# A hybrid decoder step on one core: inverse roots from a table, the last products on two engines, projection copies on ScalarE, and gathers of activations issued earlier

## The reference, cut to what matters

```
h = RMSNorm(x);  q, k, v, gates = h @ w_in
x += (sigmoid(gate_a) * attention @ w_a + sigmoid(gate_r) * retention @ w_r) @ w_o
h2 = RMSNorm(x)
x += PEER(h2)          # 128*128 = 16384 experts; 8 heads * 16 picks per token:
                       #   a = gelu(u[pick] . h2) * gate;  x += sum a * v[pick]
x += sigmoid(RMSNorm(x) @ w_ple_gate) * (p @ w_ple_proj)     # p: 256 wide
y = RMSNorm(x)
```

## Time and profile before

| | us |
|---|---|
| median of 3 runs (4647.2 to 4655.68) | 4655.38 |
| the profiled execution, its own time | 4651.09 |
| span from its first to its last instruction | 4649.5 |
| PE busy | 4572.7 (98%) |
| DVE busy | 2908.9 (63%) |
| ACT busy | 1241.7 (27%) |
| POOL busy | 1410.9 (30%) |
| mean granted TensorE clock | 0.994 |

### The profile page before, as it was taken

The page is one execution under the profiler, slowest core; times in us unless marked ns, Lnnn a source line. Parts: engine busy times, 40 slices in busy tenths (PEclk is TensorE's granted clock), DMA queues, the critical chain, the costliest instruction groups (busy, mean ns, idle before and its releaser), DMA issues.

```text
span 4649.5 us, 83246 instructions
## 1 busy us (share of the span) xinstructions
PE 4572.7 (98%) x33321; PEld 4501.8 (97%) x33321; DVE 2908.9 (63%) x4977; ACT 1241.7 (27%) x1636; POOL 1410.9 (30%) x1038
## 2 busy tenths in 40 slices
PE   8999999999999999999999999999999999999997
PEld 8999999989999999999999999999999999999997
DVE  7743442334425789556666525665659999999844
ACT  4113332133223122221111121212223333332332
POOL 1000000010000014443333324244147777665300
PEclk9999999999999999999999999999999999999999
DMA  6553345455544444245555478788868899999422
GB/s 216 162 168 113 115 153 170 151 164 165 176 152 131 145 134 143 104 141 172 173 170 176 169 248 277 270 303 290 313 255 334 330 373 383 377 372 352 185 81 90
DMA packets 538040, 976.03 MB, mean 210 GB/s; under 512 B 46027, under 2 KB 388315, under 8 KB 505947
## 3 DMA queue, kind: packets, MB, share of 16 engines
q1 hardware_dynamic: 185200, 471.13, 29.5%
q0 software_dynamic: 72304, 355.95, 19.8%
q10 hardware_dynamic: 280368, 146.70, 11.0%
HBM read 924.94 MB, written 230.82 MB: 249 GB/s over the span
## 4 chain that ended last, share of the span: by engine, by line
PE 89%; DVE 4%; issue 2%; DMA 2%; POOL 1%; ACT 1%; ACTq 0%; another core or an unknown queue 0%; DVEq 0%; SPq 0%; POOLq 0%
PE PS L2065 66%; PE PS L2563 18%; PE PS L2513 1%; DVE acc L1906 1%; DVE w_lo L1171 1%; DMA rows_y<-v_rows,row_iy 1%; POOL a_y L669 1%; DVE PS L1866 1%; DMA w_raw<-in_w 0%; PE PS L2457 0%; PE PS L2173 0%; ACT w_hi L761 0%; PE PS L2199 0%; ACTq L796 0%; DVE h_lo L1195 0%
## 5 line engine op out<-in xcount | busy, mean ns | idle before, releaser
L2065 PE MATMUL PS<-h_hi,w_hi 128*128 128x288 f32 x7808 | 2328.0, 298 | 31.0 <-DVE w_lo L1171 18.7
L2065 PE MATMUL PS<-h_lo,w_hi 128*128 128x288 f32 x7808 | 2306.1, 295 | 0.9 <-issue 0.9
L2065 PE MATMUL PS<-h_hi,w_lo 128*128 128x288 f32 x7808 | 2306.0, 295 | 0.7 <-issue 0.6
L2065 PEld LDWEIGHTS PS<-h_hi,w_hi 128*128 128x128 f32 x7808 | 1470.0, 188 | 62.9 <-issue 35.9
L2065 PEld LDWEIGHTS PS<-h_hi,w_lo 128*128 128x128 f32 x7808 | 1471.5, 188 | 1.0 <-issue 1.0
L2065 PEld LDWEIGHTS PS<-h_lo,w_hi 128*128 128x128 f32 x7808 | 1471.2, 188 | 1.4 <-issue 0.5
L761 ACT ACTIVATE w_hi<-w_raw 128x1024 fp32r<-128x1024 f32 x522 | 553.4, 1060 | 2438.2 <-PE PS L2065 2314.5
L1171 DVE TENSOR_TENSOR w_lo<-w_raw,w_hi 128x1024 fp32r<-128x1024 f32 x372 | 458.8, 1234 | 765.5 <-ACT w_hi L761 727.1
L625 POOL TENSOR_TENSOR w_lo<-w_raw,w_hi 128x1024 fp32r<-128x1024 f32 x152 | 379.0, 2493 | 1030.3 <-ACT w_hi L761 1030.3
L699 POOL DMA_INDIRECT a_el<-act_scr,act_i x192 | 322.6, 1680 | 58.9 <-issue 58.2
L1906 DVE SCALAR_TENSOR_TENSOR acc<-rows,a_sel,acc 128x2048 f32<-128x2048 f32 x128 | 301.1, 2353 | 3.9 <-POOL row_x L729 2.8
(11 more groups left out here) (353 smaller groups left out, 5375.1 us busy)
## 6 DMA issues: line engine op xcount, KB each, us to landing
w_raw<-in_w SPq DMA_DIRECT2D x652, 512.0 KB
v_rows<-in_w ACTq DMA_DIRECT2D x512, 256.0 KB, 3.8
v_raw<-in_w SPq DMA_DIRECT2D x128, 512.0 KB
act_scr<-gsp POOLq DMA_DIRECT2D x128, 288.0 KB
gate_scr<-g_st POOLq DMA_DIRECT2D x12, 2048.0 KB, 8.6
gl<-act_scr SPq DMA_DIRECT2D x20, 640.0 KB
fu_a<-act_scr SPq DMA_DIRECT2D x19, 640.0 KB
fu_g<-gate_scr SPq DMA_DIRECT2D x19, 640.0 KB
```

Of the source, the lines that this page charges most:

```text
L2065: ins = mm(dst[:, a], w[:, m, at + n], xx[:, k, a * TH:(a + 1) * TH], start=first and n == 0 and r == 0, stop=last and n == len(ks) - 1 an ...
```

## The change

Five edits:

1. Roots. In `root(2)` and `root(3)` ACT computes `Abs_reciprocal_sqrt` in place of `Sqrt`, and DVE's reciprocal goes; the three Newton instructions stay. In `root(3)` a fourth instruction writes the same result into PSUM as well, ahead of the one that writes `rstd2` and raises the new semaphore `rooted`.
2. Last products. DVE multiplies tiles 0 to 11, with the factor read from PSUM; POOL multiplies tiles 12 to 15, with the factor from SBUF. SP stores the pairs in the order 0, 1, 6, 2, 3, 7, 4, 5.
3. Projection copies. DVE copies the even tiles, ACT the odd ones (semaphore `p_done`), and PE waits for each by its own semaphore. ACT's splits stand at k = 1, 3, 5, 9 in place of 4, 8, 12, 15; DVE's low parts move up with the fewer copies.
4. Picks 32 to 47 are issued in iterations 96 and 97 in place of 97 and 98.
5. Within every POOL iteration of chunks 76 to 127 the picks come ahead of the rows in place of behind them. The iterations that have both are 84 to 87, 100 to 103 and 106 to 109, with four picks each.

```diff
 PICK_AT = {80: (0, 8), 81: (8, 16), 84: (16, 20), 85: (20, 24), 86: (24, 28), 87: (28, 32),
-           97: (32, 40), 98: (40, 48), 100: (48, 52), 101: (52, 56), 102: (56, 60), 103: (60, 64),
+           96: (32, 40), 97: (40, 48), 100: (48, 52), 101: (52, 56), 102: (56, 60), 103: (60, 64),
            106: (64, 68), 107: (68, 72), 108: (72, 76), 109: (76, 80), 110: (80, 84), 111: (84, 88)}
...
-            for n in range(KD // 2):
-                sp.wait_ge(S["yd"], 2 * n + 2)
+            for n in (0, 1, 6, 2, 3, 7, 4, 5):
+                if n < 6:
+                    sp.wait_ge(S["yd"], 2 * n + 2)
+                else:
+                    sp.wait_ge(S["yp"], 2 * n - 10)
                 sp.dma_start(o["y"][:, 2 * n:2 * n + 2], x[:, 2 * n:2 * n + 2]).then_inc(S["out"], 16)
...
                 put_gated(t)
+                for n in range(*PICK_AT.get(t, (0, 0))):
+                    pick_y(n)
                 for n in range(NY):
                     if Y_AT[n] == t + 1:
...
-                for n in range(*PICK_AT.get(t, (0, 0))):
-                    pick_y(n)
...
+            pool.wait_ge(S["rooted"], 2)
+            for k in range(KD - 4, KD):
+                pool.wait_ge(S["xl"], k + 1)
+                nc.gpsimd.tensor_tensor(x[:, k], x[:, k], rstd2[:], ALU.mult).then_inc(S["yp"], 1)
...
                 square(2, k)
-                if k in (4, 8, 12, 15):
-                    split(B_PG + 1 + (k + 1) // 4)
+                if k < KD // 2:
+                    n = 2 * k + 1
...
+                    nc.scalar.activation(halves(proj[:, n]), ring_a(n), ACT.Copy).then_inc(S["p_done"], 1)
+                if k in (1, 3, 5, 9):
+                    split(B_PG + 2 + (1, 3, 5, 9).index(k))
             split(B_PG + 6)
             split(B_PG + 7)
             act.wait_ge(S["ms"], 3)
-            nc.scalar.activation(rstd2[:], rms2[:], ACT.Sqrt).then_inc(S["rt"], 1)
+            nc.scalar.activation(rstd2[:], rms2[:], ACT.Abs_reciprocal_sqrt).then_inc(S["rt"], 1)
...
                 dve.wait_ge(S["rt"], 3 if r == 2 else 5)
-                inverse_root(rstd2, rms2)
+                ch.did(v.scalar_tensor_tensor(rms2[:], rms2[:], -0.5, rstd2[:], ALU.mult, ALU.mult))
+                ch.wait()
+                ch.did(v.tensor_tensor(rms2[:], rms2[:], rstd2[:], ALU.mult))
+                ch.wait()
+                if r == 3:
+                    ch.did(v.scalar_tensor_tensor(PS[:, 2:4, 0:TH], halves(rms2[:]), 1.5, halves(rstd2[:]), ALU.add, ALU.mult))
+                v.scalar_tensor_tensor(rstd2[:], rms2[:], 1.5, rstd2[:], ALU.add, ALU.mult).then_inc(S["rooted"], 1)
+                dve.wait_ge(S["rooted"], r - 1)
...
-            for n in range(KD):
+            for n in range(0, KD, 2):
                 projected(n)
-                if n >= 3 and n % 2 == 1:
-                    low_part((n - 3) // 2)
-                if n in (5, 9, 13):
+                if n >= 2:
+                    low_part(n // 2 - 1)
+                if n in (4, 8, 12):
                     split(B_PG + 2 + n // 4 - 1)
...
             root(3)
-            for k in range(KD):
+            ch.wait()
+            for k in range(KD - 4):
                 dve.wait_ge(S["xl"], k + 1)
-                v.tensor_tensor(x[:, k], x[:, k], rstd2[:], ALU.mult).then_inc(S["yd"], 1)
+                v.tensor_tensor(halves(x[:, k]), halves(x[:, k]), PS[:, 2:4, 0:TH], ALU.mult).then_inc(S["yd"], 1)
```

More of the change, by code:

```diff
@@ L354, in build @@
         names = """raw0 raw1 hi lo used free_a free_b vt const ones x0 x1 x2 x3 x4 x5 x6 x7 x_again s0 s0_out gn0 gn1 gab0 gab1
-            p p_done spill0 spill1 gput0 gput1 out win_out kv_out sp_out chain passed passed_pe passed_act
+            p p_done spill0 spill1 gput0 gput1 out win_out kv_out sp_out chain passed rooted yp
             hk ms rt hf hhi h_done rope tr_k tr_v trf_k trf_v
@@ L1131, in _ @@
                 square(2, k)
-                if k in (4, 8, 12, 15):
-                    split(B_PG + 1 + (k + 1) // 4)
+                if k < KD // 2:
+                    n = 2 * k + 1
+                    if n % 4 == 1:
+                        act.wait_ge(S["vt"], 8 * NS + 3 * (n // 4) + 2)
+                    else:
+                        act.wait_ge(s_used, B_PG + n // 4 + 1)
+                    nc.scalar.activation(halves(proj[:, n]), ring_a(n), ACT.Copy).then_inc(S["p_done"], 1)
+                if k in (1, 3, 5, 9):
+                    split(B_PG + 2 + (1, 3, 5, 9).index(k))
             split(B_PG + 6)
@@ L1154, in _ @@
                 if t == KD - 1:
-                    nc.scalar.activation(part[:], part[:], ACT.Sqrt).then_inc(S["rt"], 1)
+                    nc.scalar.activation(part[:], ones[:, 0:1], ACT.Abs_reciprocal_sqrt).then_inc(S["rt"], 1)
                 else:
@@ L1985, in projected @@
                 q, m = n // 4, n % 4
[L1986 to L1989, removed]
+                dve.wait_ge(S["vt"], 8 * NS + 3 * q + m + 1)
                 v.tensor_copy(halves(proj[:, n]), ring_a(n)).then_inc(s_free_a, 1)
@@ L2600, in _ @@
                 for m in range(4):
-                    pe.wait_ge(s_free_a, A_PG + 4 * q + m - 1)
+                    n = 4 * q + m
+                    if n % 2 == 0:
+                        pe.wait_ge(s_free_a, A_PG + n // 2)
+                    else:
+                        pe.wait_ge(S["p_done"], 2 + n // 2)
                     if q == 0 and m == 1:
@@ L2606, in _ @@
             full_tile(ring_b(0), B_PG + 4, h_hi, h_lo, h0=4 * KD)
-            pe.wait_ge(s_free_a, A_PG + KD)
+            pe.wait_ge(s_free_a, A_PG + KD // 2)
+            pe.wait_ge(S["p_done"], 2 + KD // 2)
             pe.wait_ge(S["ssq"], 3 * (KD - 1))
```

## The result

The changed kernel takes 4673.97 us in the median of 5 runs (4668.72 to 4676.22), the kernel before 4655.38 us (4647.2 to 4665.81 in 5 runs). The ratio is 1.0039 with a 95% interval of [1.0022, 1.0056]: slower by 18.6 us, outside the forecast range of 4641 to 4667, and on the side to which 0.19 was given. The profiled execution took 4673.97 us, its span is 4672.1 us and its mean granted clock 0.990; before it was 4651.09, 4649.5 and 0.994.

The account below looks back on a forecast made before the run. PE is busy 98% of the span, so only its waits and the tail can give time. Tail -3.1, projections and first root -3.0, strip +4.3 sum to -1.8 us: 4653.5 us against 4655.38, range 4641 to 4667.

Parts of the forecast that it names:

- The order of picks and rows: Strip of chunks 83 to 111: picks ahead delay the first row 5.04 us, adding PE waits for splits.
- the ring: Loop through POOL and DVE (store, picks, row landing, product, split, `gated`): 16.7 us against 12.7 for a chunk.
- 16.5 - (12.2 - 5.7): Strip: 13.6 + 2.9 = 16.5 us with the change, against 12.2 before; 5.7 is the earlier picks' gain.
- L = 6.5: Strip: landing time in us taken for a gathered row, near the first of two rows (6.3 and 8.3).
- eight listed turns: Strip turns 85, 87, 88, 101, 103, 104, 108, 109: a row's product stands ahead of the next iteration's second split.
- a rival of its own at +1.6 to +3.4: Low clock stays at the first root or follows the new stalls: 4655 to 4657 us, chance 0.07.
- The carry: Loop steps carried from turn 83 to 123: stalls of 7.9, 13.6, 20.6, 29.2 us at L 5.8, 6.5, 7.2, 8.0.
- the second rival: Strip: picks hold the rows back in a saturated DMA; at L = 8.0 +13.8 us in all, 4669; chance 0.19.
- Picks 32 to 47 an iteration earlier: Strip: DVE's wait for `a_y`, PE's 4.02 us wait at 3053 and the low clock go: -5.7 us.
- Second root and last products: Tail: reciprocal goes (-3.76), PSUM result added (+0.67), split of the products gives 0: -3.1 us.
- the third rival: Tail: the PSUM factor doesn't free DVE's products from POOL's: +2.9 us, total +1.1, 4656.5; chance 0.07.
- Projections and first root: Projections: copy waits go, low parts wait on POOL's adds, root's chain 3.78 us shorter: sum -3.0 us, bounds -6 and +1.

Follow-up runs that it names:

- a2_picks_96: Kernel before with only picks 32 to 47 moved to iterations 96 and 97: 4640.73 us, ratio to before 0.998.
- c3_two_engines: Kernel before plus roots by look-up, picks 32 to 47 earlier, last products on two engines with PSUM factor: 4633.47 us, ratio to before 0.9973.
- a1_rows_first: Kernel after with POOL issuing an iteration's rows ahead of its picks again: 4634.66 us, ratio to before 0.997.
- b3_no_mid: Kernel after, picks still ahead of rows, but no row product between an iteration's two splits: 4645.5 us, ratio to before 0.9983.
- c2_half_picks: Kernel after with half of an iteration's picks ahead of its rows and half behind: 4639.62 us, ratio to before 0.9983.

## Why the prediction was wrong

**The order of picks and rows: the ring right, two terms of its size wrong, and so were most of its places.** The forecast priced it at 16.5 - (12.2 - 5.7) = +10.0 us; it costs 28.7 and 29.5.

The first step that failed is the choice of L = 6.5, near the shorter of two rows, because "the rows start 5 us later, when the chunk's other transfers are mostly done". All eight listed turns have a first product that waited for its row in the kernel before; from issue to product they took 5.8 to 9.2 us, 7.9 in the mean, so the row of 6.3 was a short one. In the kernel after seven of these products waited. Their rows took 5.5 to 9.2 us, 7.7 in the mean, where the same seven had taken 8.1: the later start was worth some 0.4 us, not the 1.4 between 7.9 and 6.5. Turn 85 of the kernel after, then turn 109 of the kernel before (POOL and DVE):

```profile
2849.93 1.00 POOL L679 DMA_INDIRECT rows_y<-v_rows,row_iy  x1 [0.30 <-issue]
2858.04 2.36 DVE L1880 SCALAR_TENSOR_TENSOR PS<-rows_y,a_y,PS 128x2048 f32<-128x2048 f32 x1 [9.23 <-DMA rows_y<-v_rows,row_iy]
```

```profile
3164.86 1.04 POOL L676 DMA_INDIRECT rows_y<-v_rows,row_iy  x1 [0.30 <-issue]
3174.06 2.35 DVE L1866 SCALAR_TENSOR_TENSOR PS<-rows_y,a_y,PS 128x2048 f32<-128x2048 f32 x1 [4.30 <-DMA rows_y<-v_rows,row_iy]
```

The DMA engines were not empty for the late rows: 372 GB/s from 3189.5 to 3198.0, share 1.09, and more than half of the 3.16 MB moved in it (1.68) were other transfers than the rows.

The second wrong term is the larger. Both the forecast and the rival priced new waits at their own length. The waits in the strip came out at 21.1 us where I had 16.5: 4.6 missed. The products were slow for 13.5 us (426.28 less 412.8, the 414.51 of before without its 1.7) where I had none, 11.8 of it behind waits. I had used the rule on the waits that go (4.02 + 1.7, 2.51 + 1.6) and not on those that come, except as a rival of its own at +1.6 to +3.4. It belonged into each case that has waits of 2 us and more: at 11.8 / 21.1 = 0.56 us for each us waited, the forecast's own 16.5 us carry 9.2 more, and its sum is +7.4 instead of -1.8.

The places came out in part. The six products for which DVE waited longest (9.55, 9.23, 7.33, 6.73, 6.59 and 6.58 us) stood in turns 109, 85, 101, 104, 108 and 88, all in the list. But of the four chunks at which I expected PE to wait, 89, 104, 105 and 110, only 110 has its wait behind the product that I named. PE waited at chunks 86, 88, 102, 104, 107 and 110, and not at all behind the products of turns 88, 103 and 104. The carry left out that products behind both splits, in turns 86 and 102, hold up the next iteration's first split, and it priced too high as well: at L = 7.7 it gives about 26 us (between its 20.6 and 29.2), more than the strip's 21.1. So the second rival, which said that the rows would not land faster and gave 4669 us with L = 8.0, was right on the landing, but came near the time by luck: it had 32.1 us of waits and no slow products, where there were 21.1 and 13.5.

**Picks 32 to 47 an iteration earlier: right.** DVE's `a_y` no longer waits, PE's 4.02 us at chunk 100 are gone in every kernel with the edit; -5.7 forecast, -6.3 (some 2 either way) from the means, and `a2_picks_96` as a whole lies between -14 and -5 us.

**Second root and last products: right.** -3.1 forecast; `c3_two_engines` has -3.15 (23.74 to 20.59). The kernel after has -2.4, since its last sum ran at the low clock (2.02 us in place of 1.24 for its four products). In all seven kernels that have the projections part with full adds the low stretch reaches into that sum (1.66 to 2.29 us), in the other seven it takes 1.24 to 1.33; why it starts earlier there stays open. The PSUM factor frees the products, so the third rival falls. The rule of the Trainium skill, SBUF — State Buffer, "Who interferes with whom", holds on both sides: 12.92 us with two SBUF inputs, 8.06 with one in PSUM. (That rival's price had a slip: from the last product to the end it is 4649.5 - 4645.5 = 4.0 us, not 3.8, so +3.0 and not +2.9.) The split of the products is worth zero, as forecast, and with the copy of the root that it needs it loses 0.67 us, which the forecast had in its sum. The better choice was to leave it out.

**Projections and first root: the sum near, its parts not.** -3.0 forecast; -1.4 in the kernel after, 241.0 us (-3.0) in `a1_rows_first` and in `b3_no_mid`. But the root alone brings -4.3, and the split of the copies by itself -0.3; on top of the shorter root it costs 1.3 to 2.9. The step that failed is the waits for low parts: I had 2.7 + 0.7 + 3 x 1.15 = 6.9 us without a low clock, they were 2.30 + 0.83 + 0.83 = 4.0 us with one or two low stretches (and 5.2 us with none in `c2_half_picks`, to the same 241.0). "A low stretch at 4416 to 4426 instead would cost little, since PE waits for low parts there" was wrong, because most of the low stretch lies behind the wait, where PE works.

**The sum.** With the means: order +29.5, picks -6.3, roots -8.1, two engines +0.7, projections +2.1 (mean of 1.3 and 2.9), last sum at the low clock about +0.8: +18.7 us. The medians differ by 18.6. That they agree to 0.1 is luck: each strip alone scatters by several us, and the 29.5 is itself read from the strip of the kernel after.

## What to carry to other kernels

Before a transfer is moved behind others on its queue, follow its consumer: if the consumer stands ahead of something urgent on an in-order engine, the delay closes a ring (here store, picks, row, landing, product, split, `gated`), and what counts is by how much the ring exceeds the loop's period against the slack in front of the urgent work, not the delay by itself: here half of it was nearly free, all of it cost 29 us. Look also at the work behind the urgent point, which is ahead of the next one. Don't count on a later start for a quicker landing where the DMA is busy: here it was worth 0.4 of 8.1 us. Take such a time from all rows of the kind that the trace has, not from two. And price a wait of TensorE that comes with the slow products behind it, in every case and not in one of the rivals: here they added about as much as the waits (10.1 and 9.6 us).

## What the runs showed of the hardware

Between chunk 80 and the last sum, the 14 executions profiled have 92 waits of TensorE of 1 us or more. A low stretch (0.50, in pieces of 3.4 us) began within 9 us (how far I looked) of the start of 2 of 40 waits of 1 to 2 us, of 29 of 41 of 2 to 4 us, and of all 11 of 4 us or more; 9 of these 11 were followed by two pieces, 6.8 us. So for waits of 2 to 4 us the length alone doesn't tell the cost, and this can be part of the scatter between kernels that run the same instructions. And not every low stretch comes behind such a wait: of the 61 in these executions 19 have none in the 9 us before them. Ten of the 19 begin 1.6 to 3.0 us behind the eviction of chunk 112, seven at 3004 to 3020; what brings them stays open.

POOL is held up too: beside DVE products with two SBUF inputs its own took 1.9 us each (7.58 for four), beside those with one in PSUM 1.41.
